# Where the stages of a Trainium2 decoder layer meet: the order of VectorE and ScalarE work, and a final RMSNorm of the last rows from squares of the transposed x

## The reference

```python
x += 0.5 * SwiGLU_1(rms(x))                    # 1024 -> 2816 -> 1024
h  = rms(x); q, k, v, u = split(h @ w_in)
x += concat(stick_breaking(q, k, v), pool(u)) @ w_out
x += CrossAttn(rms(x), rms(mem))               # 4 heads, 256 memory tokens
x += 0.5 * SwiGLU_2(rms(x))
y  = rms_final(x)                              # stored by rows of tokens
```

## Time and profile before

| | before |
|---|---|
| median of 3 runs | 2045.06 us |
| the profiled execution | 2047.72 us |
| its span, first to last instruction | 2045.9 us |
| PE busy | 97% |
| DVE, ACT, POOL busy | 65%, 42%, 28% |
| DMA | 190.15 MB, 93 GB/s on average |
| mean granted TensorE clock | 0.992 |

### The profile page before, as it was taken

One profiled execution on the slowest core, in us unless ns is written; L12 is line 12 of the kernel. 1 busy time (PEld: TensorE's weight loads), 2 busy tenths in 40 slices (PEclk: granted clock), 3 DMA queues, 4 the chain that ended last, 5 costly groups with the idle time before them and its releaser, 6 DMA issues. The chain is left out here.

```text
span 2045.9 us, 25158 instructions
## 1 busy us (share of the span) xinstructions
PE 1976.6 (97%) x9345; PEld 1627.2 (80%) x9345; DVE 1333.8 (65%) x1813; ACT 862.0 (42%) x1523; POOL 577.2 (28%) x424
## 2 busy tenths in 40 slices
PE   6999999999999899989999999999999999999997
PEld 5788888887887688766688888877788888878885
DVE  6756556559798632387655655568656556579896
ACT  6433333434445311277634444444443443434443
POOL 1345555530002122055321100221555455410000
PEclk8999999999999999999999999999999999999999
DMA  4223223235500222544134322140322322265102
GB/s 145 77 73 98 82 68 99 83 146 187 182 11 11 67 85 90 142 95 103 32 103 136 112 83 62 56 116 15 113 83 73 93 83 73 72 252 170 62 1 83
DMA packets 216466, 190.15 MB, mean 93 GB/s; under 512 B 7532, under 2 KB 171928, under 8 KB 216344
## 3 DMA queue, kind: packets, MB, share of 16 engines
q1 hardware_dynamic: 216256, 188.51, 30.0%
q10 hardware_dynamic: 88, 0.02, 0.0%
HBM read 152.85 MB, written 35.65 MB: 92 GB/s over the span
## 5 line engine op out<-in xcount | busy, mean ns | idle before, releaser
L1829 DVE TENSOR_TENSOR w_lo<-st,w_hi 128x512 fp32r<-128x512 f32 x160 | 173.5, 1086 | 178.6 <-ACT w_hi L1407 178.6
L950 PE MATMUL ps<-T_hi,w_lo 128*128 128x512 f32 x640 | 249.1, 389 | 0.3 <-issue 0.3
L951 PE MATMUL ps<-T_lo,w_hi 128*128 128x512 f32 x640 | 249.0, 389 | 0.0
L952 PE MATMUL ps<-T_hi,w_hi 128*128 128x512 f32 x640 | 249.0, 389 | 0.0
L950 PE MATMUL ps<-tr_hi,sr_lo 128*128 128x512 f32 x616 | 241.9, 393 | 5.1 <-DVE xT L2060 2.7
L952 PE MATMUL ps<-tr_hi,sr_hi 128*128 128x512 f32 x616 | 239.8, 389 | 0.0
L951 PE MATMUL ps<-tr_lo,sr_hi 128*128 128x512 f32 x616 | 239.8, 389 | 0.0
L950 PE MATMUL ps<-B_hi,w_lo 128*128 128x512 f32 x576 | 227.0, 394 | 10.9 <-DVE B_lo L1829 4.5
L951 PE MATMUL ps<-B_lo,w_hi 128*128 128x512 f32 x576 | 225.9, 392 | 0.0
L952 PE MATMUL ps<-B_hi,w_hi 128*128 128x512 f32 x576 | 225.7, 392 | 0.0
L950 PE MATMUL ps<-act_hi,wb_lo 128*128 128x512 f32 x384 | 152.3, 397 | 3.1 <-DVE wb_lo L1829 1.6
(11 more groups left out here) (257 smaller groups left out, 4220.4 us busy)
## 6 DMA issues: line engine op xcount, KB each, us to landing
gate_raw<-in_ffn_w_gate SPq DMA_DIRECT2D x44, 512.0 KB, 5.3
up_raw<-in_ffn_w_up SPq DMA_DIRECT2D x44, 512.0 KB, 5.1
h_spill<-up_s SPq DMA_DIRECT2D x66, 256.0 KB, 2.0
piece_A<-in_ffn_w_down SPq DMA_DIRECT2D x32, 512.0 KB, 4.5
piece_B<-h_spill SPq DMA_DIRECT2D x32, 512.0 KB, 6.0
wa_raw<-in_w_in SPq DMA_DIRECT2D x16, 512.0 KB, 4.0
wb_raw<-in_w_out SPq DMA_DIRECT2D x16, 512.0 KB, 3.8
wb_raw<-in_mem_w_kv SPq DMA_DIRECT2D x16, 512.0 KB, 3.8
```

The source lines that it names most:

```text
L950: pe.matmul(to, w_lo, m_hi, start=first, stop=False, skip_group_check=joins)
L951: pe.matmul(to, w_hi, m_lo, start=False, stop=False, skip_group_check=joins)
L952: return pe.matmul(to, w_hi, m_hi, start=False, stop=last, skip_group_check=joins)
L1829: return dve.tensor_tensor(to, value, plain(hi), ALU.subtract)
```

## The change

The diff moves work in the queues of ACT, DVE and PE, and replaces the final norm of four row blocks. Its parts:

1. **Entry of FFN 1.** The dummy activation that opens ACT's work is a Sqrt instead of a Square. Chunk 2 of x is copied by ACT instead of DVE. The four gate pieces are split one at a time among the copies and the first scaled chunks; PE starts after two of them (`FIRST_ORDER`), with the third and fourth waited for at d = 4. The up pieces are split on ACT before `norm_std(1)` and before the x copies of the second half; PE waits for them two by two. SP's wait for the fourth gate piece stays.
2. **m = 2.** `weight_hi(r, 2, 3)` goes behind the copy-out of s1, in both FFNs.
3. **Adds of group 11** come one step earlier, in the first FFN only.
4. **Norm 2 and 3.** `xn(2, 5..7)` and `xn_hi(2, 7)` go ahead of `norm_var(3)`/`norm_std(3)`. The first two q/k units are emptied after `xn(3, 5)` instead of `xn(3, 1)`.
5. **B_STEPS.** "tot 4" comes after mk tiles 0 and 1. The first o1 tile waits for head 2's values at its start and for head 3's at chunk 6.
6. **Entry of FFN 2.** Two up pieces are split on DVE before `norm_var(7)`/`norm_diag(7)`, two after.
7. **The end.** Rows 2 and 3 are turned after step 72. For rows 4 to 7 ACT squares the chunks of xT as they are added, POOL adds five of them up, PE sums the rest over partitions with ones (`late_sums`), one root and one Newton step serve all four row blocks, and DVE scales and SP stores halves of 512 features from a buffer of their own. The transposes of chunks 4 to 7 go ahead of the last adds.

```diff
-        XN3_FIRST = 1
+        XN3_FIRST = 5
+        LATE_SQ = (4, 5, 6, 7, 0, 1, 2, 3)
+        LATE_BY_POOL, LATE_BANK = HT + 1, 3
-        X_BY_ACT, X_BANKS = (6, 7, 4, 5), (1, 3, 4, 5)
+        X_BY_ACT, X_BY_DVE, X_BANKS = (6, 2, 7, 4, 5), (0, 1, 3), (1, 3, 4, 5)
...
-            B_STEPS += tiles("mk", j, j + 1) + [("tot", 4)] * (j == 0) + tiles("mk", j + 1, j + 2)
+            B_STEPS += tiles("mk", j, j + 2) + [("tot", 4)] * (j == 0)
...
-            g = max([g for g in range(13) if last_of[g] + (3 if g == 11 else 4) <= e], default=None)
+            after = [(2 if r == 0 else 3) if g == 11 else 4 for g in range(13)]
+            g = max([g for g in range(13) if last_of[g] + after[g] <= e], default=None)
...
@@ GpSimd
+            total = sq_all[:, LATE_SQ[0], :]
+            for n in range(1, LATE_BY_POOL):
+                pool.wait_ge(s_late_sq, n + 1)
...
+                pool.tensor_tensor(total, total, sq_all[:, LATE_SQ[n], :], ALU.add).then_inc(s_late_sum, 1)
@@ TensorE, first_pair
-                pe.wait_ge(c_wlo, 8 * r + 4)
+                pe.wait_ge(c_wlo, 8 * r + 2)
...
+                    if d == QC:
+                        pe.wait_ge(c_wlo, 8 * r + 4)
...
-                pe.wait_ge(c_wlo, 8 * r + 8)
                 for i in range(2):
+                    pe.wait_ge(c_wlo, 8 * r + 6 + 2 * i)
...
-                    if r == 1 and e == 74:
+                    if r == 1 and e == 72:
                         y_turn(2)
                         y_turn(3)
...
+            def late_sums():
+                for j in range(HT):
+                    for n in (0, *range(LATE_BY_POOL, DC)):
+                        mm = pe.matmul(ps[:, LATE_BANK, 2 * j:2 * j + 2],
+                                       sq_all[:, LATE_SQ[n], j * P:(j + 1) * P], ones[:, 0:2],
+                                       start=n == 0, stop=n == DC - 1)
...
                 if kind == "o1" and j == 0:
-                    pe.wait_ge(b_free, b_first[pv_step(2 * MHEADS - 1)] + HD)
+                    pe.wait_ge(b_free, b_first[pv_step(2 * MHEADS - 2)] + HD)
...
+                    if kind == "o1" and j == 0 and d == HD * (MHEADS - 1):
+                        pe.wait_ge(b_free, b_first[pv_step(2 * MHEADS - 1)] + HD)
...
             ffn(1)
-            for t in range(HT, TC):
-                y_turn(t)
+            for t in (4, 5):
+                pe.wait_ge(s_y, t - 1)
+                y_turn(t, (1,))
+            pe.wait_ge(p2_add, added(1, 13, 1))
+            y_turn(6, (1,))
+            pe.wait_ge(p2_add, 2 * ADDS_ALL)
+            y_turn(4, (0,))
+            y_turn(5, (0,))
+            pe.wait_ge(s_late_sum, LATE_BY_POOL - 1)
+            pe.wait_ge(s_late_sq, DC)
+            late_sums().then_inc(s_late_tot, 1)
+            y_turn(6, (0,))
+            y_turn(7, (0,))
+            pe.wait_ge(s_fvar, HT + 1)
+            y_turn(7, (1,))
@@ ScalarE
-                weight_hi(r, 2, 3)
...
                             copy_out(r, m, p, "s1")
+                            if m == 2:
+                                weight_hi(r, m, 3)
...
-            act.activation(x_sq[:, 0:1], ones[:, 0:1], ACT.Square).then_inc(s_row_sq, 1)
+            act.activation(x_sq[:, 0:1], ones[:, 0:1], ACT.Sqrt).then_inc(s_row_sq, 1)
...
+                if n == 1:
+                    act.wait_ge(s_gains_ps, 1)
+                    copy(gains[:], ps[:, 0, 0:GP + NG]).then_inc(s_gains, 1)
+                    first_hi(0, 0, 0)
+                elif n == 2:
+                    first_hi(0, 0, 1)
...
+            for n in range(4):
+                first_hi(0, 1, n)
             norm_std(1)
             for n in range(DC):
                 x_copy(n)
-            first_hi(0, 1)
...
+            xn_hi(2, 7)
             norm_std(3)
-            xn_hi(2, 7)
...
+            for n, c in enumerate(LATE_SQ):
+                act.wait_ge(p2_add, added(1, 12 + n // HT, n % HT))
+                act.activation(sq_all[:, c, :], xT[:, c, tok(1)], ACT.Square).then_inc(s_late_sq, 1)
@@ VectorE
             norm_var(0)
             x_copy(0)
+            norm_diag(0)
+            first_lo(0, 0, 0)
+            dve.wait_ge(s_gains, 1)
+            xn_scaled(0, 0)
+            first_lo(0, 0, 1)
+            xn_lo(0, 0)
             x_copy(1)
...
+            for c in range(2, DC):
                 xn(0, c)
+                if c == 3:
+                    first_lo(0, 0, 2)
+                    first_lo(0, 0, 3)
             norm_var(1)
             norm_diag(1)
...
-            xn(2, 5)
+            for c in range(5, DC):
+                xn(2, c)
             norm_var(3)
-            xn(2, 6)
             norm_diag(3)
-            xn(2, 7)
...
-            first_lo(1, 1)
+            first_lo(1, 1, 0)
+            first_lo(1, 1, 1)
             norm_var(7)
             norm_diag(7)
+            first_lo(1, 1, 2)
+            first_lo(1, 1, 3)
...
+            for n in range(2 * HT):
+                t, half = HT + n // 2, slice(n % 2 * HALF, (n % 2 + 1) * HALF)
+                dve.wait_ge(s_yT, t + 1)
+                dve.scalar_tensor_tensor(out=y_late[:, t - HT, half], in0=ps[:, Y_BANK[t] + n % 2, :],
```

More of the change, by code:

```diff
@@ L821, in _ @@
                          .broadcast_to([P, D])).then_inc(s_fin_in, 16)
-            for t in range(TC):
+            for t in range(HT):
                 sp.wait_ge(s_y, t + 1)
                 sp.dma_start(out[0, t * P:(t + 1) * P, :], y_row[:, t % 2, :]).then_inc(s_out[t % 2], 16)
+            for n in range(2 * HT):
+                t, half = HT + n // 2, slice(n % 2 * HALF, (n % 2 + 1) * HALF)
+                sp.wait_ge(s_y, HT + n + 1)
+                sp.dma_start(out[0, t * P:(t + 1) * P, half], y_late[:, t - HT, half]).then_inc(s_out[n % 2], 16)
             for slot in range(2):
-                sp.wait_ge(s_out[slot], 16 * TC // 2)
+                sp.wait_ge(s_out[slot], 16 * (HT // 2 + HT))
         @block.gpsimd
@@ L1154, in ffn, with y_turn @@
                         y_turn(1)
-                    if r == 1 and e == 74:
+                    if r == 1 and e == 72:
                         y_turn(2)
                         y_turn(3)
[L1159 to L1167, removed]
+            def y_turn(t, parts=(0, 1)):
+                if t < HT:
+                    pe.wait_ge(p2_add, ADDS_ALL + adds_before[12 if t < 2 else 13])
+                for part in parts:
+                    for c in range(4 * part, 4 * part + 4):
+                        mm = pe.transpose(ps[:, Y_BANK[t] + part, (c % 4) * P:(c % 4 + 1) * P],
+                                          xT[:, c, t * P:(t + 1) * P], ident[:])
+                if len(parts) == 2 or (parts == (0,)) == (t != TC - 1):
+                    mm.then_inc(s_yT, 1)
+            def late_sums():
[4 more added lines that the diff above has]
+                                       start=n == 0, stop=n == DC - 1)
+                return mm
             pe.wait_ge(s_gains, 1)
@@ L1437, in weight_hi, with first_hi @@
                 copy(wide_block(w_hi[p][:]), src).then_inc(p1_whi, 1)
-            def first_hi(r, which):
+            def first_hi(r, which, n):
+                i, j = FIRST_ORDER[which][n]
                 act.wait_ge(p1_in[which], 32 * (PAIRS * r + 1))
[L1441 to L1444, removed]
+                copy(wide_block(w_hi[C_SLOT[which, i, j]][:]),
+                     wide_block(raw_in[which][:, i, QC * j:QC * (j + 1), :])).then_inc(c_whi, 1)
             def second_hi(r, n):
@@ L1569, in _ @@
             norm_std(0)
[L1570 removed]
+            for n, c in enumerate(X_BY_ACT):
                 act.wait_ge(s_xt_ps, c + 1)
                 copy(xT[:, c, tok(0)], ps[:, c, :]).then_inc(s_xt_a, 1)
[L1573 to L1575 removed]
+                if n == 1:
[4 more added lines that the diff above has]
+                    first_hi(0, 0, 1)
             def x_copy(n):
@@ L1765, in _ @@
                 elif step[0] == "ffn":
-                    first_hi(1, 0)
+                    for n in range(4):
+                        first_hi(1, 0, n)
                 elif step[0] == "tot":
@@ L1791, in _ @@
             act.wait_ge(b_out, n_units)
-            first_hi(1, 1)
+            for n in range(4):
+                first_hi(1, 1, n)
             norm_std(7)
@@ L1818, in _ @@
             row_std(3)
-            row_mean(HT)
-            for t in range(HT, TC):
-                if t + 1 < TC:
-                    row_mean(t + 1)
-                row_std(t)
+            for n, c in enumerate(LATE_SQ):
+                act.wait_ge(p2_add, added(1, 12 + n // HT, n % HT))
+                act.activation(sq_all[:, c, :], xT[:, c, tok(1)], ACT.Square).then_inc(s_late_sq, 1)
+            act.wait_ge(s_fvar, HT + 1)
+            act.activation(fstat[:, 2, HT:TC], fstat[:, 1, HT:TC], ACT.Sqrt).then_inc(s_fstd, 1)
         @block.vector
@@ L2317, in _ @@
                 elif step[0] == "ffn":
-                    first_lo(1, 0)
+                    for n in range(4):
```

(18 more changed lines are left out.)

65 lines of the change are left out of this document (37 added, 28 removed).

## The result

The changed kernel took 2028.85 us, the median of 3 executions (2027.59, 2028.85, 2028.87), against 2045.06: a ratio of 0.9902, 95% interval 0.9886 to 0.9918. The forecast was 2025.0, within 2018.5 to 2034.0. The profiled execution took 2028.85 us, with a span of 2027.1, where the one before took 2047.72 with 2045.9.

A forecast was written before the change was run, and what follows sets the result against it. PE was busy 1976.6 of 2045.9 us, so reordering DVE and ACT work could win only within 69 us of standing. Eight terms summed to 19.9 us, giving 2025.2 against the median; forecast 2025.0, range 2018.5 to 2034.0 (8 in 10).

The forecast's parts named there:

- Entry of FFN 1: First FFN's start: first product near 15.9, second part at 37.4; gain 5.4 us, between 3.0 and 7.2.
- the second low stretch: Entry of FFN 1, 41.9 to 45.3 us: half-clock stretch behind the 3.98 us gap, costing 1.7, counted as gone.
- m = 2: Both FFNs: PE's 1.17 us wait for the s1 copy goes; 2.4 us in all, between 1.8 and 2.8.
- Group 11: First FFN: adds one step earlier start 2.0 us sooner; gain 1.3 us, between 0.5 and 2.0.
- Norm 3: First q/k pair: waits in norm_var(3) and for act_lo shrink, 3.7 us; 3.5 net with the moved emptying.
- tot 4, o1, norm 7, the end: B_STEPS waits at tot 4 and o1, norm before FFN 2, final norm: gains of 1.0, 1.7, 1.6 and 3.0 us.
- The sum: Whole kernel: the terms add to 19.9 us; 2027.8 against the profiled execution, 2025.2 against the median, said 2025.0.
- The signs: Profile after: products near 16 and 37 at full clock, named waits gone, under 1.5 us at group 12, last add within 1.
- signs of being wrong: Profile after: w_lo, diag or act_lo heading PE's waits, a 1.8 us split before one, low clock beyond 30 us.
- POOL takes its share back: Rival at entry, group 11, norm 3, FFN 2: moved work meets POOL's sums; 13.7 gained, 2031.4; chance 0.15.
- The early start: Rival: entry's 5.4 comes to nothing before m = 3 and m = 2 waits reopen; 12.1 left, 2033; chance 0.08.
- low clock lasted through the entry: Rival, entry: clock stays low as chunks come one by one; 19.9 lost, up to 2055; chance 0.04.

The follow-up runs named there:

- E11: Changed kernel with the dummy activation that opens ACT's work a Square again instead of Sqrt: 2028.90 us, one execution.
- E3: Changed kernel with POOL's first sum of the first FFN waiting for norm 1's diagonal: 2027.05 us, ratio 0.9902.
- E6: Changed kernel with two q/k units emptied after xn(3, 1) again and POOL's first sum behind norm 1's diagonal: 2026.06 us, ratio 0.9894.
- E4: Changed kernel with ACT splitting the first FFN's four up pieces behind the eight x copies again: 2032.47 us, ratio 0.9928.
- E10: Changed kernel with the ACT split of product 3's m = 2 weights at the end of the entry again, both FFNs: 2032.76 us, one execution.
- E8: Changed kernel with the adds of group 11 three steps behind it again in the first FFN too: 2031.38 us, one execution.
- E1: Changed kernel with the first two q/k units emptied after xn(3, 1) again: 2027.19 us, 0.99 of before.
- E9: Changed kernel with norm_var(3), norm_diag(3) between xn(2, 5..7) and norm_std(3) ahead of xn_hi(2, 7) again: 2033.43 us, one execution.
- E5: Changed kernel run again with no edit: 2028.53 us, 2025.79 to 2030.46 in five executions; ratio 0.991.

## Why the prediction was right, and where it was off

**What bounds the kernel** was read rightly: DVE and ACT work in the wrong order at eight places, and most gave what their own row said, the last four to 0.3 us. Two readings were off. The largest waits of PE in total are not the splits but those for aT among the scores, 8.6 and 5.7 us, which the earlier trace rows does not show. And the 69 us of standing does not bound the gain: a low stretch lies in PE's busy time, and the entry gained by one that went.

**Entry of FFN 1**, 5.4 forecast, 5.92 measured. The first product is at 15.96 where "near 15.9" was said; the table load was worth its 0.84 (E11: 0.76 to 0.95). The second part was put at 37.4 because one row showed a small operation of 1.25 us; it came at 36.80. The Trainium skill (SBUF — State Buffer, section Who interferes with whom) says that a DVE operation with two SBUF inputs, or one in a two-port mode, and a POOL operation that reads SBUF shut each other out for a whole instruction. The trace agrees: 1.25, 0.84 and 1.15 us beside sums of 1.70, 1.30 and 1.29, and 0.16 to 0.17 each without them (E3); no row shows the mode of the two that have one input. By that rule the prediction had 37.7, without it 35.6; the kernel of E6, where nothing meets, began at 35.28. So POOL cost 1.5 of the 2.1 us named. The 1.7 for the second low stretch was right: the table shows 1.58 between 4.34 and 5.92, and E4 brought the stretch back together with the wait, for 1.37 us.

**m = 2**, 2.4 forecast, 1.9 measured. The wait went for the full 1.4, but 0.4 to 0.5, not 0.2, is given back in the products behind it (E10).

**Group 11**, 1.3 forecast, 0.83 measured. The adds came 2.0 us sooner as said, and the splits behind them fell into POOL's sums as said (1.78 us); the cover of 5.4 us was not quite enough, and PE waits 0.86 for tr_lo. E8 could not show the price, because the clock fell there.

**Norm 3**, 3.5 forecast, 2.3 measured. The first pair gave 3.60 of the 3.7. The step that failed is the next sentence, "3.5 net": the moved emptying was priced by DVE's work alone, 0.2 us, and that is what it costs when the clock holds (0.12 by E1 against E3, E8, E9 and E11). What was left out is that it gathers two shorter waits into one of 2.14 us, behind which the clock fell in this execution, for 1.17 us more. The prediction had itself looked at waits of 2.74 and 1.66 with no fall behind them and counted on it; E8 shows a fall behind the first of these, and E9 one behind the 1.51 just ahead of the second.

**tot 4, o1, norm 7, the end**: 1.0, 1.7, 1.6 and 3.0 forecast, 1.04, 1.73, 1.83 and 3.26 measured. At the end each part stands where it was put: the adds follow the products (they wait for PE again), `late_sums` takes 3.63 us for the 3.5 said, the eight halves 5.36 for 5.3.

**The sum** was 19.9, the spans give 18.8, and the two profiled executions 18.87. That is 1.0 of the 3.85 us by which 2025.0 missed. Another 2.66 is the last step, where the sum was set against the median of three instead of the profiled execution, and 0.2 is the rounding down to 2025.0. (The ends that are written for the terms add up to 14.1 and 23.9, not 13.7 and 24.1; for tot 4 and o1 none are written.) By the groups in E5 this median fell among the fastest executions of the kernel before, with the highest clock where one is on record: all 22 of the kernel before have a median of 2047.8, the 8 of the changed one 2028.7, 19.1 apart.

**The signs** that were named came: the products near 16 and 37, no low clock at the second, no wait at the places of the earlier trace rows and of the first pair, under 1.5 us at group 12, the last add 0.7 us behind the last product. Two of the signs of being wrong came as well, a diag and act_lo among PE's waits again and a split of 1.8 us ahead of one, and they mark norm 1, the second pair and group 11.

**The rivals.** "POOL takes its share back" happened in two of its four places, for 1.5 us at norm 1 and, by the forecast less what was measured, 0.5 at group 11, not for its full 6. The early start was not swallowed: 4.34 us became 5.92 at m = 2. No low clock lasted through the entry.

## What to carry to other kernels

Price a stage by the lag of one and the same matmul in two traces, and the whole by many executions: the median of three can lie 2.7 us off when low clock stretches come and go. When work is reordered on a full engine, look at how long each single wait of PE becomes, not only at their sum: here the clock fell far more often behind waits over 2 us. Keep small operations on a critical chain clear of another engine's long ones that lock them out: one waiting instruction on POOL, which had 40 us to spare, gave PE 1.4 us.

## What the runs showed of the hardware that was not expected

The same wait at the same place is followed by a low stretch in one execution and not in the next: the 2.1 to 2.2 us one in the second pair in 5 of 9 profiles, the 2.7 us one at group 12 in E8 and not before, the 1.5 us one of norm 3 in E9 and not before. Over the thirteen profiles, from 25 us to the end of the last FFN, the clock falls within 1.6 us of the end of 9 of the 14 waits of 2.1 us and more, and of 1 of the 27 of 1.25 to 1.7 us. Yet long waits are not all: among the scores the clock falls behind pairs of waits of 0.6 to 1.2 us. A stretch of 3.4 us costs 0.8 to 1.2 us in the second pair (E10, the first profile) and 1.6 among the scores.

The low stretch around the first product, which the prediction read as the level of the start, is a fall too: the transposes of x ahead of it run 0.21 us apart up to 7.9 us and 0.11 behind, so the array had already been at the higher level. It lasts 3.4, 6.8 or 10.2 us (E5, the first profile, E3). The shortest gained nothing, since PE then waits for DVE's chunks (37.00 against 36.80); the longest also covered the spread of the first norm, which took 1.98 us instead of 1.10 and so made most of the 1.09 us by which the first product was late.

The lock between DVE and POOL works both ways: in E3 the POOL sum that began 0.17 us behind the first of four DVE splits took 3.45 us, the next one 1.28. The Trainium skill (SBUF — State Buffer, section Who interferes with whom) says that the order of issue decides who stands; here DVE came first and POOL stood, and for what was left of all four splits (2.3 us), not of one.
